# Moving the gate, norm and layout work of a delta rule into the projection that feeds it

## What is computed

```python
h = rms_norm(x, norm_w)
proj = h @ w_in            # q, k, v, z, beta, decay, sw_q, sw_k, sw_v, sw_z
# gated delta rule (4 heads of 128 channels, chunks of 64 tokens, two directions)
qkv = silu(centred_depthwise_conv(concat(q, k, v), conv_w))    # 5 taps
q = l2_norm(q) * 128 ** -0.5
k = l2_norm(k)
beta = sigmoid(beta_logit)
g = -exp(a_log) * softplus(decay_logit + dt_bias)
# in each chunk: g = cumsum(g), decay = exp(g_i - g_j),
# m = (k * beta) @ k.T * decay, its triangular inverse, u, w, a_intra,
# then a scan over the 16 chunks that carries a 128 x 128 state for each head
```

## Time and profile before

| | us |
|---|---|
| median of 3 runs | 2875.87 (2873.85 to 2876.28) |
| the profiled execution, whole | 2896.45 |
| its span, first to last instruction | 2894.7 |
| PE busy | 2475.9 (86%) |
| PE weight loads busy | 1899.5 (66%) |
| DVE busy | 1199.8 (41%) |
| ACT busy | 753.1 (26%) |
| POOL busy | 338.6 (12%) |
| mean granted TensorE clock | 0.885 of full speed |

### The profile page before, as it was taken

One profiled execution on the slowest core, in us unless ns is written; L12 is line 12 of the kernel. 1 busy time (PEld: TensorE's weight loads), 2 busy tenths in 40 slices (PEclk: granted clock), 3 DMA queues, 4 the chain that ended last, 5 costly groups with the idle time before them and its releaser, 6 DMA issues. The chain is left out here.

```text
span 2894.7 us, 40291 instructions
## 1 busy us (share of the span) xinstructions
PE 2475.9 (86%) x16889; PEld 1899.5 (66%) x16918; DVE 1199.8 (41%) x1710; ACT 753.1 (26%) x1507; POOL 338.6 (12%) x306
## 2 busy tenths in 40 slices
PE   4999848889688696999769699956849999999998
PEld 3888727888456584888544255624648787787886
DVE  3762263444366623111191165554234334243343
ACT  3121141221333313111220445502233222122121
POOL 2000002333300214000040000014230000000000
PEclk7999977999878697999875699957979999999999
DMA  4122200000335312122200300002011111111112
GB/s 150 51 64 83 87 27 2 3 3 3 120 117 189 116 44 80 44 87 87 69 2 0 133 1 1 1 0 87 15 44 49 42 57 34 54 51 39 57 36 81
DMA packets 167088, 160.01 MB, mean 55 GB/s; under 512 B 12200, under 2 KB 146044, under 8 KB 166676
## 3 DMA queue, kind: packets, MB, share of 16 engines
q1 hardware_dynamic: 161134, 137.71, 14.8%
q0 software_dynamic: 5360, 19.92, 1.8%
q10 hardware_dynamic: 438, 0.12, 0.0%
HBM read 129.33 MB, written 28.31 MB: 54 GB/s over the span
## 5 line engine op out<-in xcount | busy, mean ns | idle before, releaser
L232 ACT ACTIVATE w_hi<-w_stage 128x1024 fp32r<-128x1024 f32 x144 | 152.2, 1057 | 683.4 <-PE proj_acc L251 225.2
L249 PE MATMUL ffn_acc<-m_hi,w_hi 128*128 128x512 f32 x704 | 275.8, 392 | 43.9 <-DVE w_lo L237 43.9
L237 DVE TENSOR_TENSOR w_lo<-w_stage,w_hi 128x1024 fp32r<-128x1024 f32 x144 | 175.4, 1219 | 254.1 <-ACT w_hi L232 254.1
L250 PE MATMUL ffn_acc<-m_lo,w_hi 128*128 128x512 f32 x704 | 275.3, 391 | 0.0
L251 PE MATMUL ffn_acc<-m_hi,w_lo 128*128 128x512 f32 x704 | 275.2, 391 | 0.0
L2545 DVE SCALAR_TENSOR_TENSOR hidden<-ffn_acc,hidden_conv,hidden 128x1023 f32<-128x1023 f32 x88 | 112.8, 1282 | 271.3 <-ACT hidden L2506 264.8
L249 PEld LDWEIGHTS ffn_acc<-m_hi,w_hi 128*128 128x128 f32 x704 | 132.9, 189 | 73.4 <-DVE w_lo L237 45.9
L249 PE MATMUL proj_acc<-m_hi,w_hi 128*128 128x512 f32 x400 | 160.9, 402 | 19.8 <-POOL m_lo L1518 19.8
L249 PE MATMUL acc<-h_hi,w_hi 128*128 128x512 f32 x432 | 169.2, 392 | 4.8 <-DVE h_lo L484 4.8
L251 PE MATMUL acc<-h_hi,w_lo 128*128 128x512 f32 x432 | 168.6, 390 | 0.0
L250 PE MATMUL acc<-h_lo,w_hi 128*128 128x512 f32 x432 | 168.6, 390 | 0.0
(11 more groups left out here) (342 smaller groups left out, 4636.2 us busy)
## 6 DMA issues: line engine op xcount, KB each, us to landing
w_stage<-in_w_in SPq DMA_DIRECT2D x48, 512.0 KB, 4.1
w_ada<-in_w_ada SPq DMA_DIRECT2D x12, 2048.0 KB, 7.6
w_stage<-in_w_up SPq DMA_DIRECT2D x44, 512.0 KB, 3.8
w_stage<-in_w_out SPq DMA_DIRECT2D x16, 512.0 KB, 4.8
conv_in<-spill SPq DMA_DIRECT2D x4, 2048.0 KB, 17.0
m_resid<-resid_spill SPq DMA_DIRECT2D x2, 4096.0 KB, 13.4
spill<-y_tok POOLq DMA_DIRECT2D x16, 512.0 KB, 4.5
w_stage<-in_w_down SPq DMA_DIRECT2D x16, 384.0 KB, 3.4
```

Of the source, the lines that this page charges most:

```text
L232: nc.scalar.activation(w_hi[:, slot], w_stage[:, slot], ACT.Copy).then_inc(w_hi_ready, 1)
L237: nc.vector.tensor_tensor(w_lo[:, slot], w_stage[:, slot], w_hi[:, slot].bitcast(F32), ALU.subtract).then_inc(w_lo_ready, 1)
L249: nc.tensor.matmul(acc[:, h, :], w_hi[:, slot, k, :], hi[:, k, tok], start=k == 0, stop=False)
L250: nc.tensor.matmul(acc[:, h, :], w_hi[:, slot, k, :], lo[:, k, tok], start=False, stop=False)
```

## The change

The gates' block is projected first, as block 0; q, k and v follow as 1 to 12, then z as 13 to 16, the attention's z as 17 to 20, its q as 21 to 24, and its k and v as 25 and 26. The stage `delta_prepare` goes. Its results are made inside `project1`, by token (tokens on the partitions), between the blocks. q and k are no longer multiplied by their norms: the logarithms of the norms are added to the logarithms of the gates, which the delta rule exponentiates anyway. The running sums become matmuls with masks of ones (`c_sums`, a new constant of 320 KB). The hardware loops over blocks become straight code on all engines.

What each engine gets inside `project1`:

- PE: after block 1, 8 transposes of 16 x 128 (`turn_gates`). After each of the blocks 13 to 20, two groups of 4 transposes of 128 x 128 (`turn_kv`). After each of the blocks 18 to 21, two groups of 8 matmuls, each with a 128 x 128 slice of squares as weights and one moving column (`square_sums`). After block 23, 5 matmuls (`decay_sums`). After block 25, 16 transposes in bf16 (`turn_rows`).
- ACT: the 16 copies of the transposed k and v, 8 squares of 128 x 1024 (in blocks 17 to 20), a table load after block 20, and Exp and Ln of small tiles in blocks 21 to 25, with two copies of 72 x 1024.
- DVE: some 30 small instructions on tiles of at most 128 x 128 in blocks 2 and 20 to 24, and one at the end.
- SP: three constant loads among the weight loads, the last behind a wait for the first 8 transposed groups. POOL: one memset.

The transposed k and v share the memory of `resid`, which is stored to DRAM before them. `delta_steps` is the same but for the places of its scales, and PE no longer waits there for constants. The core of the diff:

```diff
-        DOUBLE = range(17, 21)
+        DOUBLE = range(21, 25)
...
+        Z_BLK, SWZ_BLK, SWQ_BLK, SWK_BLK, SWV_BLK = 13, 17, 21, 25, 26
...
+        KV_GROUPS = [(1, tt) for tt in range(TT)] + [(0, tt) for tt in range(TT)]
+        def groups_at(c):
+            return range(2 * (c - Z_BLK), 2 * (c - Z_BLK) + 2) if Z_BLK <= c < Z_BLK + 8 else ()
+        def squares_at(c):
+            return range(2 * (c - SWZ_BLK), 2 * (c - SWZ_BLK) + 2) if SWZ_BLK <= c < SWZ_BLK + 4 else ()
...
+                for c in range(2, SWZ_BLK):
+                    load_weights(sp, c, w_in_v[:, :, (c - 1) * P:c * P], c % 2)
+                const_load(sp, "step", s_dnc)
+                const_load(sp, "late", s_dnc)
...
+                    if b == 2:
+                        sp.wait_ge(s_tt, TT)
+                        sp.dma_start(sums_const, t["c_sums"]).then_inc(s_dnc, 16)
...
+                def turn_gates():
+                    pe.wait_ge(acc_free, 3)
+                    for tt in range(TT):
+                        mm = nc.tensor.transpose(row_bank[:, tt * 16:tt * 16 + 16], raw[0:16, 0, 2 + tt * P:2 + (tt + 1) * P],
+                                                 ident[0:16, 0:16])
+                    mm.then_inc(s_rturn, 1)
+                def turn_kv(g):
+                    which, tt = KV_GROUPS[g]
+                    pe.wait_ge(s_silu_free, 2 + (N_CONV if which else 8))
+                    if g >= 3:
+                        pe.wait_ge(s_tte, g - 2)
+                    for h in range(DN_HEADS):
+                        mm = nc.tensor.transpose(turned[g % 3][:, h * P:(h + 1) * P],
+                                                 conv_in[:, (8 if which else 4) + h, tt * P:(tt + 1) * P], ident)
+                    mm.then_inc(s_tt, 1)
+                def square_sums(i):
+                    pe.wait_ge(s_gtok, 1)
+                    pe.wait_ge(s_hq, i + 1)
+                    for tt in range(TT):
+                        mm = nc.tensor.matmul(row_bank[:, tt * 8 + i:tt * 8 + i + 1],
+                                              head_square[:, i % 2, tt * P:(tt + 1) * P], ones[:, 0:1], start=True,
+                                              stop=True)
+                    mm.then_inc(s_hqs, 1)
...
-                with pe.Fori(1, 13) as i:
-                    for s in range(2):
-                        multiply_block(pe, 2 * i + s, s, acc[s], h_hi, h_lo)
-                multiply_block(pe, 26, 0, acc[0], h_hi, h_lo)
+                turn_gates()
+                pe.wait_ge(s_ln, 2)
+                for c in range(2, C1):
+                    multiply_block(pe, c, c % 2, acc[c % 2], h_hi, h_lo)
+                    for g in groups_at(c):
+                        turn_kv(g)
+                    for i in squares_at(c - 1):
+                        square_sums(i)
+                    if c == 23:
+                        decay_sums()
+                    if c == 25:
+                        turn_rows()
...
+                def copy_kv(g):
+                    which, tt = KV_GROUPS[g]
+                    act.wait_ge(s_tt, g + 1)
+                    if g == 0:
+                        act.wait_ge(s_resid_sp, 16)
+                    nc.scalar.activation(kv_tok[:, which, tt].rearrange("p h d -> p (h d)"), turned[g % 3][:, :], ACT.Copy
+                                         ).then_inc(s_tte, 1)
+                def square(i):
+                    if i >= 2:
+                        act.wait_ge(s_hqs, i - 1)
+                    else:
+                        act.wait_ge(s_tt, TT)
+                    nc.scalar.activation(head_square[:, i % 2, :], conv_in[:, square_head(i), :], ACT.Square
+                                         ).then_inc(s_hq, 1)
...
+                    elif c == SWQ_BLK - 1:
+                        dve.wait_ge(s_gtok, 1)
+                        gate_magnitudes()
+                    elif c == SWQ_BLK:
+                        decay_logs()
+                    elif c == 23:
+                        token_args_of()
+                        row_split()
+                    elif c == 24:
+                        dve.wait_ge(s_tokq, 12)
+                        place_args()
...
-        with nc.Block(name="delta_prepare") as block:
...
-                pe.wait_ge(s_dnc, 48)
                 pe.wait_ge(s_state0, 2)
                 keep_busy(idle[:, :], 24)
```

More of the change, by code:

```diff
@@ L80, in shape_constants @@
     late = np.broadcast_to(late[:, :, None], (P, 2, DN_HEADS, 2, CH))
[L82 to L88, removed]
+    same = half[:, None] == half[None, :]
+    sums = np.stack([same & (p[:, None] <= p[None, :]), same & (p[:, None] >= p[None, :]), same,
+                     np.repeat(half[:, None] == 0, P, 1), np.repeat(half[:, None] == 1, P, 1)], 1).astype(f)
     one_unit = np.tile(np.eye(CH, dtype=f), (2, 1))
@@ new lines, in square_sums, with decay_sums @@
+                def square_sums(i):
[6 more added lines that the diff above has]
+                    mm.then_inc(s_hqs, 1)
+                def decay_sums():
+                    pe.wait_ge(s_dnc, 48)
+                    pe.wait_ge(s_tte, 2 * TT)
+                    pe.wait_ge(s_dlog, 3)
+                    for d in range(2):
+                        nc.tensor.matmul(turned[0][:, d * 32:(d + 1) * 32], sums[:, d, :],
+                                         decay_log[:, :, d * 4:(d + 1) * 4], start=True, stop=True)
+                    mm = nc.tensor.matmul(turned[0][:, 64:128], sums[:, 2, :], decay_log[:, :, :], start=True, stop=True)
+                    for hf in range(2):
+                        mm = nc.tensor.matmul(turned[1][:, hf * 64:(hf + 1) * 64], sums[:, 3 + hf, :], decay_log[:, :, :],
+                                              start=True, stop=True)
+                    mm.then_inc(s_gsum, 1)
@@ L376, in _, with turn_rows @@
+                def turn_rows():
+                    pe.wait_ge(s_part, 6)
+                    pe.wait_ge(s_cdec, 1)
+                    for a in range(2):
+                        dst = turned[1 + a][:, :].bitcast(BF16)
+                        for tt in range(TT):
+                            mm = nc.tensor.transpose(dst[0:72, tt * P:(tt + 1) * P], row_tok[:, a, tt, 0:72], identb)
+                        mm.then_inc(s_rtok, 1)
                 pe.wait_ge(s_const, 16 * 2)
@@ L447, in _ @@
                 act.sem_inc(s_silu_free, 2)
[L448 to L456, removed]
-                    split_hi(act, c + 2, c % 2, loads(c + 2))
-                    n = SILU_BLOCKS.get(c)
-                    if n is not None:
+                def copy_kv(g):
[8 more added lines that the diff above has]
+                        act.wait_ge(s_hqs, i - 1)
+                    else:
+                        act.wait_ge(s_tt, TT)
+                    nc.scalar.activation(head_square[:, i % 2, :], conv_in[:, square_head(i), :], ACT.Square
+                                         ).then_inc(s_hq, 1)
+                split_hi(act, 2, 0, loads(2))
+                for c in range(1, C1):
+                    split_hi(act, c + 2, c % 2, loads(c + 2))
+                    if c <= N_CONV:
+                        j = c - 1
+                        act.wait_ge(s_conv, j + 1)
+                        nc.scalar.activation(conv_in[:, j, :], tap_sum[:, j % 2, :], ACT.Silu).then_inc(s_silu_free, 1)
+                    elif c in SILU_BLOCKS:
+                        n = SILU_BLOCKS[c]
                         act.wait_ge(acc_free, c + 3)
@@ L508, in _ @@
                             ins.then_inc(s_tap if k < DN_TAPS - 1 else s_conv, 1)
[L509 to L522, removed]
```

453 lines of the change are left out of this document (193 added, 260 removed).

## The result

The changed kernel takes 2850.4 us (median of 6 runs, 2833.3 to 2856.2) where the kernel before takes 2876.1 (6 runs): the ratio is 0.9889, interval 0.9851 to 0.9926. A later set of 15 runs of the kernel before and 5 of the changed kernel gave 2879.0 and 2850.6 us, ratio 0.9896 (0.9851 to 0.994). It is faster by about 1%, 26 us by the first medians and 32 by the first ratio. The forecast was 43.6 us and 2832.3. The median lies 1.4 us above the upper end of the range; the ratio, put on the median that the forecast started from (2875.87), gives 2844 us, inside it.

The account below looks back on a forecast made before the run. PE alone bounds the projection's later blocks, while no engine is full in `delta_prepare`. 2896.45 - 80.6 + 27 + 10 = 2852.9 us, 43.6 less; from the median, 2875.87 - 43.6 = 2832.3 us, range 2816 to 2849.

Parts of the forecast that it names:

- The stage that goes: `delta_prepare` disappears and the end of `project1` leads straight to the memset of `delta_steps`: 80.6 us go.
- What comes on PE: Transposes, square sums, `decay_sums` and seams inside `project1`, all on the path: 27 us added.
- the two bounds: `turn_gates` and `turn_rows`, 24 smaller transposes: 0.114 us each from above, 0.030 from below; 2.7 us taken, at least 0.7.
- The seams: Some 19 insertion places in `project1`, each leaving at most one load open: 0 to 4 us, 1 taken.
- The clock: Four `square_sums` stretches after blocks 18 to 21: three falls of the clock taken, 3.4 us each, 10 us.
- the row at 883: Earlier trace, one-column matmuls: clock at 0.50 from 883.75 to 890, read as a fall of about 6.8 us costing 3.4.
- The rival without a fall: The clock does not fall at the square sums in the projection: 2822 us, chance 0.27.
- the one with four: Transposes count as pauses too, all four square-sum stretches cool the clock, 13.6 us plus 1: 2837 us, chance 0.1.
- What is hidden: New ACT, DVE, SP and POOL work in `project1` runs beside PE without making it wait: nothing added.
- the waits: Rival: PE waits for ACT or DVE at a few gaps in the projection, 8 to 16 us: 2840 to 2848, chance 0.08.
- My own sign of being wrong: The prediction is wrong if the length of `delta_steps` (328 us) moves by more than 3 us.
- the other three: Wrong if PE waits at `turn_kv` or `square_sums`, an insertion-free block exceeds 11 us, or a one-column matmul is not 0.23.

Follow-up runs that it names:

- the second trace of before: The kernel before, unchanged, traced a second time: 2891.6 us, with `delta_steps` at 328.6.
- the three long executions: Traced executions of the changed kernel with 96 unused bytes ahead of the weight tiles (2853.5 us), with 224 (2847.3), and with its first loads held back (2862.5).
- 224 bytes: The changed kernel with 224 unused bytes a partition ahead of the weight tiles: timed at 2840.0 us, ratio 0.9848 to the kernel before.
- its copy with 32 bytes: The changed kernel with an unused tile of 32 bytes a partition ahead of the weight tiles: 2852.9 us (7 runs).
- the two spread versions without the fill: Changed kernel with every second `square_sums` group moved into the next block: 2835.9 us; the same plus 224 bytes ahead of weights and of m_hi: 2808.0 us.
- the fill: Fastest spread version plus 4 dummy matmuls on PE after each of six levels of the first chunk pair in `delta_steps`: 2817.2 us, ratio 0.9789.

## Why the prediction was right or wrong

**The stage that goes: right.** 80.6 us forecast, 80.2 measured. The memset stands 390.54 - 383.72 = 6.8 us behind the last matmul, where 6.4 was forecast; the 6.4 us in the section on the result are counted from the evacuation.

**What comes on PE: right, a little high.** Transposes: 11.77 - 10.88 = 0.89 us for eight, 7.1 us in all (7.3). Square sums at full clock: 3.63 us a stretch, 14.5 (14.7), so the row with the same shape priced them to 2%. `decay_sums` 1.2 us (12.05 - 10.88, and 1.2 forecast), `turn_rows` 1.0 and `turn_gates` about 0.7 (its 8 transposes stand between two matmuls that begin 0.92 us apart instead of 0.23; 2.7 us were forecast for the two together): the smaller transposes lie between the two bounds. The seams cost nothing beyond these (1). With the falls this is 30.9 of the 32.4 us by which the last evacuation moved; the first evacuation was 1.2 us later already (71.97 after 70.79), which also differs between executions (72.58 in the second trace of before). The 152.5 us of the earlier trace rows are 14 blocks, 13 to 26, not 12 to 26 as the prediction says; nothing in its sum hangs on that.

**The clock: the mechanism right, the size off.** Three falls, at the stretches forecast, and spreading the matmuls removed them. They cost 18.57 - 15.40 = 3.2 us, then 1.6 and 1.6, together 6.4 instead of 10: the first lasted 6.8 us and the others 3.4. I took the length of the row at 883 for all falls; that one began inside its one-column matmuls, as the fall of 6.8 us here did, and the two of 3.4 us began after them. Why a fall comes early or late is open. The rival without a fall is out; the one with four describes two of the three long executions (projections of 394.3 and 394.9 us), though they cost 9.6 us there and not its 13.6.

The rule of the Trainium skill on transposes ("TensorE: Matmul & The Clock Gate", Part 4: PE-mode transpose), that they do not count as activity for the clock, found nothing for it. At the five places where transposes stand alone no trace has a fall. In the first trace the clock fell at the three stretches that have transposes ahead of them and not at the fourth, which would agree with the rule; but the fourth fell in the three long executions, and the first passed in one of them, so a fall here does not need the transposes. That they add nothing to one is not shown, since no run took them away alone.

**What is hidden: right.** PE shows no wait in the projection. The distances in blocks 14 to 18 are 11.77, so the first `turn_kv` did not wait for the silu of block 12 either.

**Outside the change: wrong, and this is where the gain went.** I took the stages behind for unchanged, because their instructions are. The sum up to the memset was 4 us better than forecast (47.9 against 43.6). The 32 bytes by which a small tile grew then cost 11 to 14 us in `hidden_layer`, shown by putting them into the kernel before, and taken back by 224 bytes. In the second output projection the matmuls slowed from 227 to 233 ns as well, 2.5 us on its 384, but its length differs by as much between executions of one kernel (159.7 and 161.5 us). With the weights put right the ratio is 0.9848; the forecast stood for 0.9848 (2832.3 by 2875.87). That the two agree to the last digit is luck, with an interval of 0.9783 to 0.9913.

**The range.** It ended at 2849 because the waits were its worst case; the placement was not among the cases. The two groups of executions were not either: I gave the delta rule 3 us each way, from a mean clock of 0.88, where the stage differs by 10 to 16 us between executions. My own sign of being wrong, a `delta_steps` that moves by more than 3 us, came true for that reason; the other three did not. And I read from one row at 0.50 that small matmuls do not hold the clock, where the same stretch of the program runs at 0.94 in another execution.

The kernel before had shown me only its long form, and I did not ask what an execution of 2876 us looks like inside, although the profiled one was 20 us above the median. Of 18 runs of the changed kernel and its copy with 32 bytes, 6 took 2832 to 2839 us and 12 took 2850 to 2857; the forecast of 2832 is at the lower end of the shorter group. In each of the two spread versions without the fill all 4 runs lie within 11 us of each other. Why spreading keeps them there is open: 6 us are the falls, the rest was never traced in both forms.

## What to carry to other kernels

A chain of small steps on all engines is worth moving under a stage that one engine bounds, at the price of what it adds to that engine, and a row of the same shape elsewhere in the trace prices this to a few per cent. One-column matmuls are better strewn in small groups between dense ones: here groups of 16 loads met no fall of the clock in three traces, and groups of 32 met one in 23 of 28 cases. After any edit of a tile's size compare the addresses of all tiles: look at the distance between matmuls in the stages that were not edited, since 2.9% of it hung on 32 bytes here. And trace both kernels more than once before a difference in an unedited stage is given to the change.

## What was not expected of the hardware

- Back-to-back matmuls of 128 x 128 weights and 512 moving columns (fp32r) start about 227 ns apart where weights and moving operand have the same address modulo 256 and about 233 ns where they have not, at a granted clock of 1.00. It held for every pair in the 13 traces, with the moving operand 32, 128, 192 or 224 bytes on from the weights; other distances, and why it is so, were not measured.
- Some 30 us near the start of the delta rule run at 0.50 or mostly at 1.00 by the execution: in one and the same stretch of 29 us 484 or 732 matmuls, and 10 to 16 us in the length of the stage.
- A fall of the clock between dense blocks lasted 3.4 us in 15 cases and 6.8 in 8, for nearly the same work.
